# Layer 0 of a two-layer decoder trunk: the second half of Q and K by halves of the tokens, with four query tiles of the first head between its products

## What is computed

```python
h = rmsnorm(x, norm_mix[0])
proj = h @ ev_w_in[0]                                   # 1024 x 2048
q, k, v, u = jnp.split(proj, [512, 1024, 1536], axis=-1)
q = rmsnorm(q.reshape(bsz, seq, 2, 4, 64), ev_q_gain[0])   # two maps, four heads
k = rmsnorm(k.reshape(bsz, seq, 2, 4, 64), ev_k_gain[0])
ya = diff_attention(q, k, v, lam, slopes_a)    # softmax(map 0) - lam * softmax(map 1), causal, ALiBi
ya = rmsnorm(ya, ev_subln_gain[0]) * (1 - lambda_init)
yb = multiscale_pool(u, ev_pool_w[0], ev_pool_scale[0])
x = x + jnp.concatenate([ya, yb], axis=-1) @ ev_w_out[0]
x = x + swiglu_ffn(x, ...)
```

## Time and profile before

| | |
|---|---|
| median of 3 runs | 2171.35 us (2168.88 to 2172.96) |
| profiled execution | 2170.43 us |
| its span | 2168.6 us |
| TensorE busy | 2128.9 us, 98% |
| VectorE / ScalarE / GpSimd busy | 1321.8 / 900.3 / 865.6 us |

### The profile page before, as it was taken

How to read it: one execution, slowest core, us unless ns; L and a number is a source line. 1 busy time by engine, 2 the same in 40 slices (tenths; PEclk the granted TensorE clock), 3 DMA queues, 4 the chain that set the end, 5 groups by cost and what they waited for, 6 DMA issues and landing times.

```text
span 2168.6 us, 30058 instructions
## 1 busy us (share of the span) xinstructions
PE 2128.9 (98%) x10572; PEld 1774.0 (82%) x10572; DVE 1321.8 (61%) x1725; ACT 900.3 (42%) x1497; POOL 865.6 (40%) x571
## 2 busy tenths in 40 slices
PE   8999899999999999999999999999999999999999
PEld 7877798888888888788888887888888888888887
DVE  4345875775555565457597447766865565555555
ACT  4134875443333333445333137852433333334433
POOL 1022432466677663002063124320576667751000
PEclk9999999999999999999999999999999999999999
DMA  5011421055555556676402120311265554557565
GB/s 193 1 56 51 127 79 30 20 165 201 181 188 166 174 174 233 214 243 191 130 20 59 49 78 21 121 56 39 68 202 188 199 172 155 168 178 278 194 194 194
DMA packets 229534, 295.55 MB, mean 136 GB/s; under 512 B 11824, under 2 KB 133168, under 8 KB 229168
## 3 DMA queue, kind: packets, MB, share of 16 engines
q1 hardware_dynamic: 229136, 294.04, 41.4%
q10 hardware_dynamic: 288, 0.05, 0.0%
HBM read 208.06 MB, written 77.59 MB: 132 GB/s over the span
## 4 chain that ended last, share of the span: by engine, by line
PE 79%; issue 13%; ACT 3%; DVE 2%; POOL 2%; DMA 1%; SPq 0%; POOLq 0%; ACTq 0%; DVEq 0%
PE PS L1591 12%; PE PS L1592 12%; PE PS L1590 12%; PE PS L1617 6%; PE PS L1618 6%; PE PS L1619 6%; PE PS L1119 4%; PE PS L1121 4%; PE PS L1120 4%; PE PS L1203 2%; PE PS L1242 1%; POOL QRS L1009 1%; PE PS L1307 1%; PE PS L1309 1%; PE PS L1308 1%
## 5 line engine op out<-in xcount | busy, mean ns | idle before, releaser
L2198 DVE TENSOR_TENSOR LINEl<-LINE,HIGH 128x1024 fp32r<-128x1024 f32 x154 | 196.0, 1281 | 167.2 <-ACT HIGH L1648 166.8
L1648 ACT ACTIVATE HIGH<-LINE 128x1024 fp32r<-128x1024 f32 x154 | 163.1, 1060 | 236.8 <-PE PS L1619 215.7
L1617 PE MATMUL PS<-HIGH 128*128 128x512 f32 x616 | 240.9, 391 | 3.5 <-ACT KEEP L1648 3.2
L1619 PE MATMUL PS<-HIGH,LINEl 128*128 128x512 f32 x616 | 240.4, 390 | 0.0
L1618 PE MATMUL PS<-LINEl,HIGH 128*128 128x512 f32 x616 | 240.2, 390 | 0.0
L2198 DVE TENSOR_TENSOR SLOTl<-BLOCKS,RING 128x512 fp32r<-128x512 f32 x168 | 157.5, 938 | 93.1 <-ACT RING L1648 88.6
L941 POOL TENSOR_TENSOR ST<-ST 128x512 f32<-128x512 f32 x132 | 192.4, 1458 | 35.5 <-DMA ST<-in_ffn_w_down 26.8
L1648 ACT ACTIVATE RING<-BLOCKS 128x512 fp32r<-128x512 f32 x168 | 105.9, 630 | 227.7 <-PE PS L1592 221.5
L2198 DVE TENSOR_TENSOR SLOTl<-SLOT,RING 128x512 fp32r<-128x512 f32 x126 | 133.4, 1059 | 86.7 <-ACT RING L1648 86.4
L1009 POOL TENSOR_TENSOR QRS<-QMS,EXPO 128x8 f32<-128x8 f32 x32 | 52.2, 1641 | 220.6 <-DVE QMS L2459 220.1
L1617 PEld LDWEIGHTS PS<-HIGH 128*128 128x128 f32 x616 | 116.1, 188 | 28.8 <-issue 4.0
(11 more groups left out here) (426 smaller groups left out, 5716.1 us busy)
## 6 DMA issues: line engine op xcount, KB each, us to landing
LINE<-hidden SPq DMA_DIRECT2D x154, 256.0 KB, 2.7
hidden<-HID SPq DMA_DIRECT2D x44, 512.0 KB, 4.3
ST<-in_ffn_w_down SPq DMA_DIRECT2D x44, 512.0 KB, 4.1
sums<-ST SPq DMA_DIRECT2D x22, 1024.0 KB, 6.0
hidden<-ST SPq DMA_DIRECT2D x22, 1024.0 KB, 6.7
LINE<-sums SPq DMA_DIRECT2D x88, 256.0 KB, 2.9
BLOCKS<-in_ffn_w_gate SPq DMA_DIRECT2D x42, 512.0 KB, 4.0
BLOCKS<-in_ffn_w_up SPq DMA_DIRECT2D x42, 512.0 KB, 5.2
```

Of the source, the lines that this page charges most:

```text
L1617: pe.matmul(dst, hi[:, 0, ts], hi[:, 1, :], start=j == 0 and not adds_on, stop=False, skip_group_check=adds_on)
L1619: pe.matmul(dst, lo[:, 0, ts], hi[:, 1, :], start=False, stop=j == NJ - 1, skip_group_check=adds_on).then_inc(dn_pe, 1)
L1648: return nc.scalar.activation(dst, src, ACT.Copy, **kw)
L2198: return v.tensor_tensor(dst, src, hi.bitcast(F32), ALU.subtract)
```

## The change

The first half of Q and K stays. The second half of layer 0 is cut in two by tokens. First token tiles 0 to 3 go through all four weight blocks (steps 0 to 3). Then token tiles 4 to 7 do (steps 4 to 7), in the order q = 2, 3, 1, 0: blocks 2 and 3 are still in their places, blocks 1 and 0 are loaded and split a second time as r = 8 and 9, their low parts by GpSimd. Between the sixteen groups of steps 4 to 7, TensorE transposes token tiles 0 to 3 and runs query tiles 0 to 3 of head 0 completely (`EARLY = 4`), with both maps' scores in banks 0 and 1, turned tiles in bank 2 and results in bank 3, since banks 4 to 7 hold the product. The results go to a new tile `Y0`. ScalarE, VectorE and GpSimd have their work in a matching order. SP loads the tables ahead of block 6 and copies K's halves ahead of the first output weights. In `scaled` the square is written to the place of the result, and the copy waits for it. The bias of head 1 is made at tile 5, not at tile 1. Layer 1 does the same work in the same order; GpSimd's loop is written out.

The core of the diff:

```diff
+        EARLY = 4
+        def score_at(L, m, n):
+            return 512 * m if L == 0 and n < EARLY else 1024 * m
+        def y_at(n):
+            return Y0[:, n, :] if n < EARLY else Y[:, n % NT, P * (n // NT):P * (n // NT) + P]
         def weighed(n):
-            return bank(7 if n < FILL_FROM and n % 2 else 6)[:, 0:P]
+            return bank(3 if n < EARLY else 7 if n < FILL_FROM and n % 2 else 6)[:, 0:P]
...
+                for r in range(6):
+                    load_qk(r, r // 4, r % 4)
+                if L == 0:
+                    load_tables()
+                    for r, q in ((6, 2), (7, 3), (8, 1), (9, 0)):
+                        load_qk(r, 1, q)
+                    swap_keys(0)
+                    sp.wait_ge(wq_lo, WQ_AT[1])
+                    load_quarter(0)
...
                 if L == 0:
+                    for r in (8, 9):
+                        pool.wait_ge(wq_hi, r + 1)
+                        if r == 8:
+                            pool.wait_ge(qk_rs, 2 * NT - 4)
+                        nc.gpsimd.tensor_tensor(WQl[r % 2][:], RQ[r % 2][:], WQh[r % 2][:].bitcast(F32), ALU.subtract).then_inc(wq_lo, 1)
+                        pool.wait_ge(wq_lo, r + 1)
                     low_w("q0", QWl[0][:], QWs[0][:], QWh0[:])
-                    low_stacks(1, 0, 1)
+                    for n in range(2 * NT - 4, 2 * NT):
+                        qk_power(n)
+                    pool.wait_ge(qk_rs, 2 * NT)
+                    low_stacks(1, 0, 1, 2, 3)
                     low_u(2)
-                    low_stacks(1, 2, 3, 4, 5)
+                    low_stacks(1, 4, 5)
...
+                def qk_by_tokens():
+                    for step in range(4):
+                        pe.wait_ge(wq_lo, 4 + step + 1)
+                        for t in range(4):
+                            if step == 0:
+                                pe.wait_ge(bank_free[0], NT + t + 1)
+                                pe.wait_ge(mix_ok, 2)
+                            qk_group(t, step, step)
+                            if step == 0 and t < 2:
+                                mix(2 + t)
+                    pe.wait_ge(mix_ok, 4)
+                    for step, q in ((4, 2), (5, 3), (6, 1), (7, 0)):
+                        if step >= 6:
+                            pe.wait_ge(wq_lo, step + 3)
+                        for t in range(4, NT):
+                            qk_group(t, q, step)
+                            k = 4 * (step - 4) + t - 4
+                            if k < 4:
+                                qk_turn(1, k)
+                            if k == 3:
+                                both_scores(0)
+                            elif k == 5:
+                                both_scores(1)
+                            elif k == 7:
+                                both_scores(2)
+                            elif k == 8:
+                                turn(0, 0, 0, 0)
+                            elif k == 9:
+                                weigh(0)
+                                both_scores(3)
+                            elif k == 10:
+                                turn(0, 0, 0, 1)
+                            elif k == 11:
+                                weigh(1)
+                            elif k == 12:
+                                turn(0, 0, 0, 2)
+                            elif k == 13:
+                                weigh(2)
+                                turn(0, 0, 0, 3)
+                            elif k == 14:
+                                weigh(3)
+                                score(0, 0, 0, 0, EARLY)
+                    qk_turn(1, 4)
+                    score(0, 1, 0, 0, EARLY)
+                    qk_turn(1, 5)
+                    both_scores(5)
+                    qk_turn(1, 6)
+                    turn(0, 0, 0, EARLY)
+                    qk_turn(1, 7)
+                    both_scores(6)
...
                 def scaled(n):
-                    act.wait_ge(o_ok[0], n + 2)
-                    nc.scalar.activation(YJ[:], weighed(n), ACT.Square, scale=RDN[:, c:c + 1],
+                    nc.scalar.activation(y_at(n), weighed(n), ACT.Square, scale=RDN[:, c:c + 1],
                                          accum_out=YSS[:, n:n + 1]).then_inc(y_sq, 1)
-                    copy(Y[:, i, P * u:P * u + P], weighed(n), scale=RDN[:, c:c + 1]).then_inc(o_ok[0], 1)
+                    act.wait_ge(y_sq, n + 1)
+                    copy(y_at(n), weighed(n), scale=RDN[:, c:c + 1]).then_inc(o_ok[0], 1)
...
+                    for n in range(EARLY):
+                        if n + 1 < EARLY:
+                            if n > 0:
+                                dve.wait_ge(c_ok, n)
+                            biased(0, 0, 0, n + 1)
+                        for m in range(2):
+                            dve.wait_ge(s_ex[m][0], n + 1)
+                        denominators(n)
+                        if n + 1 < EARLY:
+                            biased(1, 0, 0, n + 1)
+                        ratio(n)
+                        combine(n)
```

More of the change, by code:

```diff
@@ L1378, in _, with qk_group @@
[L1378 to L1389 removed]
+                def qk_group(t, q, step):
+                    ts = slice(P * t, P * t + P)
+                    for r in range(2):
+                        last = mm3(bank(t), HH[:, 2 * q + r, ts], HL[:, 2 * q + r, ts], WQh[q % 2 if step < 6 else 1 - q % 2][:, r, :],
+                                   WQl[q % 2 if step < 6 else 1 - q % 2][:, r, :], step % 4 == 0 and r == 0, step % 4 == 3 and r == 1)
+                    if step % 4 == 3:
+                        last.then_inc(qk_pe, 1)
+                    elif step in (0, 1, 4, 5) and t % 4 == 3:
+                        last.then_inc(wq_pe[0], 1)
```

399 lines of the change are left out of this document (246 added, 153 removed).

## The result

The changed kernel takes 2178.44 us, the median of 8 runs (2175.73 to 2181.72), against 2171.35 us: ratio 1.0036, 95% interval [1.0026, 1.0046], or 7.1 us more. That is slower beyond what this measurement can tell from no change; I had forecast 2174.7 us and called "the same" the likeliest. The profiled execution of the changed kernel is the longest of its eight (2181.72 us, span 2179.9), so places inside it are compared with the kernel before, and totals by medians.

What follows compares the result with a forecast made beforehand. TensorE, busy for 98% of the span, was taken to bound the kernel, with VectorE setting the window behind the product. From 2171.35 us, +1.1 without the clock and +2.2 for the clock gave 2174.7 us; 8-in-10 range 2167.5 to 2178.5.

Steps and rivals of the forecast that it cites:

- step 1: Second half of the Q and K products: TensorE waits from 176.6 to 181.0 us for weight block 6, +4.4 us.
- step 2: Scores, transpositions and products with V of tiles 0 to 3 go ahead of the product's end, +6.5 us there.
- wait in `scaled`: The copy in `scaled` now waits for the square of the same row of Y: 0 to 1 us, taken as 0.
- step 3: Window behind the product, to tile 7's turning: VectorE sets its length and has less work, -9.8 us.
- step 4: TensorE's clock falls during the wait for block 6 and matmuls run at half pace behind it, +2.2 us.
- second low stretch: Rival's clock term: a second fall behind the gap ahead of tile 4's turn, +2.3 us; chance 0.20.
- The sum without the clock: Block 6's wait, work moved forward and the shorter window behind the product: +4.4 + 6.5 - 9.8 = +1.1 us.
- the sign that I had named: If the forecast is right, tile 7 is turned some 1 to 4 us later than 245.45.
- The second long gap: Rival: TensorE waits some 3 us ahead of tile 4's turn and the clock falls again; 2177.0 us, chance 0.20.
- the idle stretch at the kernel's end: After the last matmul the granted clock had fallen some 3.0 us after work ended; the forecast's measure for long gaps.
- the cheap tail: Rival: GpSimd's subtractions miss the combinations, window behind the product 21 us, clock stays up; 2169.1 us, chance 0.15.
- the full clock: Rival: the clock stays up through the wait for block 6; 2172.5 us, chance 0.27.

Runs made afterwards that it cites:

- fill1: Changed kernel plus 18 matmuls without use in TensorE's wait for block 6; 2176.02 us, ratio 1.0023 to the kernel before.
- fill2: fill1 plus 13 more matmuls without use in TensorE's gap ahead of the turning of tile 4; 2173.31 us, ratio 1.0013.
- y_no_wait: Changed kernel in which the copy in `scaled` no longer waits for the square just ahead of it (tiles 3 and 31 keep the wait); 2175.28 us, ratio 1.0021.
- after_sc6: Changed kernel with only the scores of tile 6 asked for ahead of the turn of tile 4; 2177.01 us, ratio 1.0025.
- k_early: best with low parts of blocks 8, 9 on VectorE, next heads' K parts behind the product's second step, output weights' low part behind tile 4's combination; 2166.64 us.
- best: Changed kernel with blocks 6, 7 split early, tile 6's scores ahead of tile 4's turn, and the `scaled` wait removed as in y_no_wait; 2168.33 us, ratio 0.9989.
- blk6_early: Changed kernel with the parts of blocks 6 and 7 made earlier, block 6's ahead of the mixer's, on ScalarE and VectorE; 2173.77 us, ratio 1.0013.
- before_g3: Kernel before with only the last output weights' high part on ScalarE moved from ahead of tile 30's turning to idle time; 2169.27 us, ratio 0.9990.
- before_with_wait: Kernel before plus one line: the copy of Y in `scaled` waits for the square ahead of it; 2172.58 us, ratio 1.0007.

## Why the prediction was wrong

Up to the turning of tile 31, 9.0 us behind the kernel before (356.19 against 347.20), the profiled execution splits as follows. The prices come from fill1, fill2 and y_no_wait, and add up to 9.0:

| part | forecast | measured |
|---|---|---|
| step 1, wait for block 6 | +4.4 | +4.4 (start to start 4.45) |
| step 2, work ahead of the product's end | +6.5 (6.0 to 7.0) | +7.5 (fill1: 223.21 - 162.00 - 49.24 - 4.45), 0.4 of it the wait in `scaled` |
| step 3, window behind the product | -9.8 (-7 to -13) | -9.9 (fill2: 24.21 against 34.08) |
| step 4, clock behind the first wait | +2.2 (0 to 5) | +2.7 (fill1); 1.7 in after_sc6 |
| second low stretch | rival, +2.3 | +1.5 (fill2) |
| wait in `scaled` | 0 (0 to 1) | +1.5 to tile 30, 0.2 at 31 |
| third low stretch, at tile 31 | not seen | +1.1 (7.82 us from turn 30 to turn 31, fill2 6.71), and 0.5 more behind turn 31 |

The sum without the clock is what failed most. Forecast was +1.1 us. Runs at full clock, of fill2 and of the kernel before, differ by 4.1 us (last section). The other 3.0 us of the median's 7.1 would then be the clock, an estimate, where the forecast had 2.2. By the sign that I had named, tile 7 was to be turned 1 to 4 us later than 245.45; it was 6.1 us later.

**Steps 1, 3 and 4 held** in mechanism, and within half a microsecond or so in size. Block 6 came as late as VectorE's queue said. The clock fell behind the long wait. I had written that no wait inside the kernel before is long enough to show that, and this was wrong: the fall behind 2.25 us at 870.16 is in that very trace, and could have warned of gaps of 2 to 3 us from the start. The windows' rule "VectorE sets the length, count its work" gave 24.3 us for 24.2. It is a good rule and not exact: in fill2 VectorE was busy for 21.30 us of the 24.21, and k_early brought the window to 21.84 with 20.59 us of VectorE's work.

**Step 2 failed in a sentence that I had treated as a footnote**: "In `scaled`, the copy now waits for the square of the same row of Y. I have no row of such a wait; between nothing and 1 us in all, I take 0." It is 0.14 us, but it stands in a loop of 32 tiles, on the engine that ends TensorE's wait in several of them, and came to some 2.1 us: 0.4 in the product, 1.5 from tile 7 to tile 30, 0.2 behind. I costed it as if it lay only in the four moved tiles. The bound was taken from nothing; a wait ended by ScalarE's copy was there to be read in the kernel before (1.58 us at 344.69), and whatever is put ahead of that copy is paid in full.

**Step 2's sum was 1 us short.** Of that, 0.36 us is the wait in `scaled` in the moved tiles. Another 0.2 us is TensorE waiting for the single bank of `weigh` even without it (tiles 2 and 3 in best); I had taken that as covered. The rest is likely what a change of shape costs: behind a transposition the second matmul of 512 columns starts 0.31 us after the first, not 0.23 (196.33 and 196.64 above). Seven such places are new in the product, 0.6 us, an estimate. No run takes these two apart.

**The second long gap was no rival but part of the likeliest case.** The forecast's sum had this fall at nothing; it cost 1.5 us. I had estimated the gap at 3 us, it was 3.23, and said it decides where it is as long as the idle stretch at the kernel's end; it was. A chance of 0.20 was too low for something of which I had both the size and the point. That rival's sum, 2177.0, with the 1.5 us of `scaled` makes 2178.5, the measured median, but by luck: it has 4.5 us of clock where the median shows some 3.0, and 2.6 us of the rest where it shows 4.1. In its stead I had let the cheap tail and the full clock take 0.42 of the chance.

The range ended at 2178.5, the median is 2178.44: inside by less than a tenth of a microsecond, and only since the second gap was among the cases. The chances were wrong in their order: slower, at 0.32, should have been first.

Not settled: when a wait of about 2 us brings the clock down (last section). At tile 30 one such fall costs 1.1 us up to the turn of tile 31 in the changed kernel and 1.6 us in fill1 and blk6_early (8.35 us between the turns, 6.71 in fill2), so a total by single executions is uncertain by 1 to 2 us for each. Matmul for matmul, the profiled execution is 9.5 us behind the kernel before once the third low stretch is over, and 11.3 us at the end. The other 1.8 us come between 1400 and 2000 us. There the profiles of the other kernels lose 0.5 to 3.0 us as well, before_g3 and before_with_wait among them, so nothing shows that they belong to the change.

## What to carry to other kernels

When a loop over more tiles is changed in one line to serve the few that move (here a semaphore wait for the sake of a new target), cost that line for all its turns, and look in the trace for waits ended by the very instruction behind it. When work is pulled ahead and its producer's queue is not reordered with it, look for the first consumer that now asks early: one block's low part, 1.2 us of work in the wrong place of VectorE's queue, cost 4.4 us of waiting and 1.7 to 2.7 us of clock. A change that turns many short waits of TensorE into a few long ones has to be priced with the clock from the start, each long wait by itself. Look through the whole trace of the kernel before for stretches of low clock first, not only near the change: here one stood behind a wait of 2.25 us.

## What the runs showed of the hardware

**A wait is paid for twice, and useless work saves the second part.** With the same arrival of block 6, 18 matmuls whose results nobody reads made the kernel 2.7 us faster at the place, and some 2.8 us in the median (1.0036 to 1.0023, with intervals that overlap). The Trainium skill, "TensorE: Matmul & The Clock Gate", Part 1, says that the array is gated to half its rate after idleness and works its way out again, and that a wait for data inside a loop can be charged for in this way each time. Three falls in one kernel agree with that.

**It takes less than one long gap, and length alone does not decide.** I had expected a fall behind 3 to 4 us. In the fourteen profiles all seven waits of 3.2 us and more inside the kernel brought the clock down, and so did all four waits of 2.2 us for the copied K. At tile 30 an idle stretch of 1.84 us was enough in five of seven profiled kernels; 1.58 us in the kernel before and 1.57 in y_no_wait were not. At the border of the layers, where none of the edits lies, the clock fell in eight, behind waits of 2.00 to 2.34 us, and stayed up in six, behind 1.69, 1.75, 2.11, 2.26, 2.26 and 2.48 us. The wait of 2.43 us ahead of 11.95, my reason for a clock that stays up, does not hold in every execution either: in fill1, k_early and before_g3 the clock was at 0.50 from 13.2 to 16.0 us, behind waits of 2.27, 2.69 and 2.41 us at that place. No run here separates the length from what the engine did around it.

**Runs at full clock lie close together.** Of the 32 runs of the kernel before in the first series, the seven with a mean granted clock of 1.000 took 2168.14 to 2169.76 us, the sixteen at 0.998 took 2168.95 to 2174.16. The seven of fill2 at 1.000 lie within 0.6 us (2172.76 to 2173.33), its one at 0.997 took 2178.44. Below 1.000 the mean clock says little about a single run: over the runs of the kernel before, its squared correlation with the time is 0.43, 0.29 and 0.29 in the three series. Runs at full clock of the one and of the other differ by 4.1 us (mean 2173.15 against 2169.04), and the table's parts without the clock, 4.4 + 7.5 - 9.9 + 1.5 + 0.2, make 3.7.

**A combination beside a GpSimd subtraction.** 640 columns took 2.00 and 2.04 us with it and 0.89 without. The Trainium skill, "Trainium Architecture — The Big Picture", "What this means for kernel authors", says that VectorE and GpSimd share a pair of ports under an exclusive lock; these rows agree as to the wait, and do not show its grain.
